# Seven of eight column blocks of each up projection as seven block products

## The reference

```python
def squared_relu_mlp(u, w_up, w_down):
    return jnp.square(jax.nn.relu(u @ w_up)) @ w_down

f = squared_relu_mlp(rmsnorm(h, norm_mlp_pre[i]), w_up[i], w_down[i])
h = h + rmsnorm(f, norm_mlp_post[i])
```

## Time and profile before

| | |
|---|---|
| median of 3 runs | 1296.06 us |
| the profiled execution | 1294.74 us, its span 1293.0 us |
| TensorE matmuls busy | 1281.8 us, 6743 matmuls |
| VectorE, ScalarE, GpSimd busy | 811.8, 656.3, 161.5 us |
| seven blocks of the up projection, layer 0 and 1 | 446.8 to 599.1 and 982.0 to 1134.3 us |
| DMA | 230.01 MB, mean 178 GB/s |

### The profile page before, as it was taken

How to read it: one execution, slowest core, us unless ns; L and a number is a source line. 1 busy time by engine, 2 the same in 40 slices (tenths; PEclk the granted TensorE clock), 3 DMA queues, 4 the chain that set the end, 5 groups by cost and what they waited for, 6 DMA issues and landing times.

```text
span 1293.0 us, 17991 instructions
## 1 busy us (share of the span) xinstructions
PE 1281.8 (99%) x6743; PEld 1058.1 (82%) x6743; DVE 811.8 (63%) x1160; ACT 656.3 (51%) x1141; POOL 161.5 (12%) x195
## 2 busy tenths in 40 slices
PE   9999999999999999999999999999999999999998
PEld 7777878888778988888888898777788888888886
DVE  5676686888544633346787974776374334478887
ACT  6645455677533423235555744775453323365663
POOL 0056353452000000000000000000000000000000
PEclk9999999999999999999999999999999999999999
DMA  7588775354864468858866527646224678669854
GB/s 247 159 269 267 219 180 152 103 165 131 219 155 99 147 198 202 217 170 217 252 207 192 183 83 174 129 108 158 66 82 122 219 182 208 227 189 246 249 173 153
DMA packets 110367, 230.01 MB, mean 178 GB/s; under 512 B 8134, under 2 KB 18646, under 8 KB 110038
## 3 DMA queue, kind: packets, MB, share of 16 engines
q1 hardware_dynamic: 84240, 159.93, 38.0%
q0 software_dynamic: 21760, 67.11, 24.0%
q10 hardware_dynamic: 4294, 2.00, 0.9%
HBM read 225.69 MB, written 70.04 MB: 229 GB/s over the span
## 4 chain that ended last, share of the span: by engine, by line
PE 93%; DVE 3%; DMA 1%; ACT 1%; issue 1%; DVEq 0%; ACTq 0%
PE G L1990 49%; PE G L2417 4%; PE G L2421 4%; PE G L2419 4%; PE X L2013 3%; PE X L2417 3%; PE X L2419 3%; PE X L2421 3%; PE G L2071 3%; PE X L2071 3%; PE X L1990 3%; PE X L2177 1%; PE X L2186 1%; PE X L2260 1%; DVE conv L1433 1%
## 5 line engine op out<-in xcount | busy, mean ns | idle before, releaser
L1296 DVE TENSOR_TENSOR wlo<-raw,whi 128x1024 fp32r<-128x1024 f32 x143 | 176.9, 1237 | 284.3 <-ACT whi L708 284.1
L1990 PE MATMUL G<-uhi,whi 128*128 128x512 f32 x736 | 294.3, 400 | 1.1 <-DVE sz L1421 0.9
L1990 PE MATMUL G<-uhi,wlo 128*128 128x512 f32 x736 | 287.1, 390 | 0.0
L1990 PE MATMUL G<-ulo,whi 128*128 128x512 f32 x736 | 286.7, 390 | 0.0
L708 ACT ACTIVATE whi<-raw 128x1024 fp32r<-128x1024 f32 x143 | 151.6, 1060 | 244.4 <-PE G L1990 159.3
L1118 ACT ACTIVATE whi<-raw 128x1024 fp32r<-128x1024 f32 x112 | 118.5, 1059 | 122.7 <-PE G L2421 52.0
L1764 DVE TENSOR_TENSOR wlo<-raw,whi 128x1024 fp32r<-128x1024 f32 x112 | 135.7, 1223 | 66.0 <-ACT whi L1118 65.6
L1990 PEld LDWEIGHTS G<-uhi,whi 128*128 128x128 f32 x736 | 138.2, 188 | 32.1 <-issue 2.0
L1990 PEld LDWEIGHTS G<-uhi,wlo 128*128 128x128 f32 x736 | 138.1, 188 | 29.6 <-DVE wlo L1344 0.2
L1990 PEld LDWEIGHTS G<-ulo,whi 128*128 128x128 f32 x736 | 138.3, 188 | 28.5
L608 POOL DMA_DIRECT2D tsum<-in_w_down x32 | 32.9, 1038 | 650.2 <-PE G L1990 536.6
(11 more groups left out here) (371 smaller groups left out, 2471.5 us busy)
## 6 DMA issues: line engine op xcount, KB each, us to landing
tsum<-in_w_down POOLq DMA_DIRECT2D x48, 1024.0 KB, 10.4
raw<-in_w_up SPq DMA_DIRECT2D x64, 512.0 KB, 3.9
raw<-tsum SPq DMA_DIRECT2D x64, 512.0 KB, 4.0
raw<-in_w_down SPq DMA_DIRECT2D x48, 512.0 KB, 4.8
raw<-in_ssd_w_in SPq DMA_DIRECT2D x20, 512.0 KB, 4.3
raw<-in_w_mem_kv SPq DMA_DIRECT2D x16, 512.0 KB, 3.7
raw<-in_ssd_w_out SPq DMA_DIRECT2D x16, 512.0 KB, 4.2
raw<-in_swa_w_in SPq DMA_DIRECT2D x16, 512.0 KB, 4.5
```

The costliest lines, as they stand in the source:

```text
L1296: dve.tensor_tensor(wlo[q][:, :, :], src[:, :, :], whi[q][:, :, :].bitcast(F32), ALU.subtract).then_inc(lo_done, 1)
L1990: mm = pe.matmul(o, st, mv, start=(kt == 0 and fresh and not go_on), stop=(q == total - 1 and k == 1), skip_group_check=True)
```

## The change

Seven of the eight column blocks (x = 0 to 6) are done with the same seven products as the down projection: tokens, contraction and columns are halved, so that a product takes 256 tokens, 512 rows and 256 columns of weights, as 2 x 4 x 3 = 24 matmuls with 256 moving columns. The left operand is a quarter of `uhi`/`ulo` for M5, M2, M3 and M6, and for M1, M4, M7 a sum of quarters (`us_parts`), made once a layer from an unsplit copy of u (`u_raw`, copied by ScalarE's `u_copy`); M6's sum is put over the fourth quarter of `uhi`/`ulo`. Sums of weights are made by VectorE in `added` or in place (`up_add`). SyncE loads four quarters of 512 rows x 256 columns a block. Even blocks use the banks G, odd ones X. The first block's relus go straight into `hid` and are squared in place. Panel numbers stay a multiple of four by letting the last product of each odd block count for two. The loads of the gains go out later, in the down products; GpSimd's sums are released at other panel numbers, at nearly the same rate. The diff, cut to its core, goes by engine: names and buffers, SyncE, ScalarE (`u_copy` to the first `up_step`), VectorE (`up_lo` to its own `up_step` and their order), TensorE:

```diff
-UP, PROD, DOWN = 8, 7, 14
-B_KV, N_KV = 39, 23
-B_QA, N_QA = 40, 24
-B_QB, N_QB = 41, 25
-B_Q1, N_Q1 = 42, 26
-B_W1, N_W1 = 43, 27
-B_F1, N_F1 = 46, 29
+PROD, UP, DOWN = 7, 14, 14
+SPLIT = 7
...
+LOADED = {M5: 0, M3: 1, M4: 2}
+ADDED = {M2: 1, M1: 2, M7: 3, M6: 4}
+W_OF, E_OF, E_FULL, W_FULL, C11, C22 = range(1, 7)
+def up_panel(x, r):
+    return 4 + 7 * x + x // 2 + r
+def up_fill(x, r):
+    return 2 if x % 2 and r == PROD - 1 else 1
+def up_next(x, r, n):
+    k = PROD * x + r + n
+    return divmod(k, PROD) if k < PROD * SPLIT else (SPLIT, k - PROD * SPLIT)
...
+        added = put("added", [P, 2, 512], F32, 88)
+        u_raw = [put(f"u_raw{i}", [P, KT, T], F32, (40, 72)[i]) for i in range(2)]
+        us_raw = [[put(f"us_raw{i}{x}", [P, 4, 256], F32, (72, 40)[i] + 4 * x) for x in range(4)] for i in range(2)]
+        us_parts = [[put(f"us{x}{p}", [P, 4, 256], F32R, 8 * x + 4 * p) for p in range(2)] for x in range(3)]
...
+        def up_bank(x, r):
+            return ((X if x % 2 else G)[{M5: 0, M3: 0, M2: 1, M4: 1, M1: 2, M7: 2, M6: 3}[r]])
...
+                def quarter(x, slot, kh, ch):
+                    c0 = 512 * (x + 1) + 256 * ch
+                    src = a["w_up"][i][512 * kh:512 * kh + 512, c0:c0 + 256].rearrange("(k p) n -> p k n", p=P)
+                    sp.dma_start(by_rows(down_raw[slot]), src).then_inc(ring_in[slot], 16)
+                for x in range(SPLIT):
+                    if x == 0:
+                        sp.wait_ge(lo_done, 4 * blk + 1)
+                    else:
+                        sp.wait_ge(up_sum, 28 * i + 4 * (x - 1) + ADDED[M7])
+                    quarter(x, 0, 0, 1)
+                    sp.wait_ge(lo_done, 4 * blk + (3 if x == 0 else up_panel(x - 1, M4) + 1))
+                    quarter(x, 2, 1, 0)
+                    if x == 0:
+                        sp.wait_ge(lo_done, 4 * blk + 2)
+                    else:
+                        sp.wait_ge(up_sum, 28 * i + 4 * (x - 1) + ADDED[M6])
+                    quarter(x, 1, 1, 1)
+                    sp.wait_ge(lo_done, 4 * blk + (4 if x == 0 else up_panel(x - 1, M7) + 1))
+                    quarter(x, 3, 0, 0)
...
+            def u_copy(i, t):
+                act.wait_ge(uhi_ready, U0[2 * i + 2] + 2 * t + 2)
+                act.wait_ge(ulo_ready, U0[2 * i + 2] + 2 * t + 2)
+                for x in range(2):
+                    cp = act.activation(u_raw[i][:, :, P * t + 64 * x:P * t + 64 * x + 64],
+                                        U_BANK[t][x][:, :].rearrange("p (k n) -> p k n", k=KT), ACT.Copy)
+                cp.then_inc(u_raw_done, 1)
...
+                def up_hi(x, r):
+                    n = 4 * blk + up_panel(x, r)
+                    if r in LOADED:
+                        act.wait_ge(ring_in[LOADED[r]], 16 * (23 * i + 2 + x))
+                    else:
+                        act.wait_ge(up_sum, 28 * i + 4 * x + ADDED[r])
+                    act.wait_ge(panel_done, n - 3)
+                    act.activation(by_rows(whi[n % 4]), up_right(r), ACT.Copy).then_inc(hi_done, up_fill(x, r))
...
+                def relu_square(x, th, ch, src):
+                    place = up_out(x, th, ch)
+                    c = 36 * i + 8 + 4 * x + {(0, 1): 0, (1, 0): 1, (0, 0): 2, (1, 1): 3}[th, ch]
+                    act.activation(place, src, ACT.Relu).then_inc(up_relu, 1)
+                    act.wait_ge(up_relu, c - 8 * i - 7)
+                    act.activation(place, place, ACT.Square).then_inc(hidsq_done, 1)
...
+                    nx, nr = up_next(x, r, LOOK)
+                    if nx < SPLIT:
+                        up_hi(nx, nr)
+                    else:
+                        right_hi(nr)
+                    if r == M5 and x > 0:
+                        up_c11_square(x - 1)
+                    elif r == M2:
+                        act.wait_ge(panel_done, 4 * blk + up_panel(x, M5) + 1)
+                        act.activation(up_out(x, 0, 0), up_bank(x, M5)[:, :], ACT.Copy).then_inc(up_m5, 1)
+                        if x > 0:
+                            up_c22_square(x - 1)
+                    elif r == M1:
+                        act.wait_ge(panel_done, 4 * blk + up_panel(x, M3) + 1)
+                        relu_square(x, 0, 1, up_bank(x, M3)[:, :])
+                    elif r == M7:
+                        act.wait_ge(panel_done, 4 * blk + up_panel(x, M4) + 1)
+                        relu_square(x, 1, 0, up_bank(x, M4)[:, :])
...
+                def up_lo(x, r):
+                    n = 4 * blk + up_panel(x, r)
+                    dve.wait_ge(hi_done, n + up_fill(x, r))
+                    dve.tensor_tensor(by_rows(wlo[n % 4]), up_right(r), by_rows(whi[n % 4]).bitcast(F32),
+                                      ALU.subtract).then_inc(lo_done, up_fill(x, r))
+                def up_add(x, r):
+                    b12, b22, b21, b11 = (by_rows(down_raw[y]) for y in range(4))
+                    out_at, other = {M2: (by_rows(added), b21), M1: (by_rows(added), b12), M7: (b11, b12),
+                                     M6: (by_rows(added), b22)}[r]
+                    first = b11 if r == M2 else out_at
+                    for y in {M2: (3, 2), M1: (0,), M7: (), M6: (1,)}[r]:
+                        dve.wait_ge(ring_in[y], 16 * (23 * i + 2 + x))
+                    if r != M2:
+                        dve.wait_ge(up_sum, 28 * i + 4 * x + {M1: 1, M7: 2, M6: 3}[r])
+                    dve.tensor_tensor(out_at, first, other, ALU.add).then_inc(up_sum, 1)
...
+                    nx, nr = up_next(x, r, LOOK)
+                    if nx < SPLIT:
+                        up_lo(nx, nr)
                     else:
-                        dve.wait_ge(panel_done, 4 * blk + 4)
-                    half_relu(1, b, X[b // 2][:, 256 * (b % 2):256 * (b % 2) + 256]).then_inc(half_free, 1)
-                def relus(f, j):
-                    c = 36 * i + 16 * f + 4 * j + 4
-                    for b in range(4):
-                        group_ready(dve, N_F[i] + 4 * f + j, 4 * (blk + 4 * f + j) + 4, b)
-                        dve.wait_ge(hidsq_done, c + b - 1)
-                        dve.tensor_scalar(og[b % 2][:, :], G[b][:, :], 0.0, None, ALU.max).then_inc(bank_free[b], 1)
-                with dve.Fori(1, 4) as j:
-                    ahead(blk + j)
-                    relus(0, j)
+                        right_lo(nr)
+                    w_at, e_at = up_out(x, 0, 0), up_out(x, 1, 1)
+                    before = 4 * blk + up_panel(x, r)
+                    if r == M5 and x > 0:
+                        up_c22_add(x - 1)
+                    elif r == M2:
+                        up_add(x, M7)
+                    elif r == M3:
+                        dve.wait_ge(panel_done, before)
+                        dve.wait_ge(up_m5, 7 * i + x + 1)
+                        dve.tensor_tensor(w_at, up_bank(x, M2)[:, :], w_at, ALU.add).then_inc(up_combined, 1)
+                        up_add(x, M6)
+                    elif r == M1:
+                        dve.wait_ge(up_relu, 28 * i + 4 * x + 1)
+                        dve.wait_ge(up_combined, 42 * i + 6 * x + W_OF)
+                        dve.tensor_tensor(e_at, up_bank(x, M3)[:, :], w_at, ALU.subtract).then_inc(up_combined, 1)
+                    elif r == M4:
+                        dve.wait_ge(panel_done, before)
+                        dve.wait_ge(up_combined, 42 * i + 6 * x + E_OF)
+                        dve.tensor_tensor(e_at, up_bank(x, M1)[:, :], e_at, ALU.add).then_inc(up_combined, 1)
+                        if x + 1 < SPLIT:
+                            up_add(x + 1, M2)
+                    elif r == M7:
+                        dve.wait_ge(up_relu, 28 * i + 4 * x + 2)
+                        dve.wait_ge(up_combined, 42 * i + 6 * x + W_OF)
+                        dve.tensor_tensor(w_at, up_bank(x, M4)[:, :], w_at, ALU.subtract).then_inc(up_combined, 1)
+                    elif r == M6:
+                        dve.wait_ge(panel_done, before)
+                        dve.wait_ge(up_combined, 42 * i + 6 * x + W_FULL)
+                        dve.tensor_tensor(w_at, up_bank(x, M7)[:, :], w_at, ALU.add).then_inc(up_combined, 1)
+                        if x + 1 < SPLIT:
+                            up_add(x + 1, M1)
+                    if x == SPLIT - 1 and r in (M4, M7):
+                        left_parts(M5, r - M4)
+                    if x >= 4 and r == M1:
+                        left_sums(1, x - 4)
...
+                for b in range(4):
+                    dve.wait_ge(half_ready, 8 * i + 2 * (b // 2) + 2)
+                    half_relu(0, b)
+                us_add(1)
+                us_add(2)
+                up_lo(0, M5)
+                up_add(0, M2)
+                up_lo(0, M2)
+                us_lo(M1)
+                up_lo(0, M3)
+                up_add(0, M1)
+                for b in range(4):
+                    if b < 2:
+                        dve.wait_ge(out_ready, 3 * N_F[i] + 2)
```

(87 more changed lines are left out.)

218 lines of the change are left out of this document (133 added, 85 removed).

## The result

| | before | after |
|---|---|---|
| median | 1295.5 us (1294.6 to 1297.4) | 1375.0 us (1372.1 to 1384.7) |
| profiled execution: span | 1293.0 us | 1370.3 us |
| TensorE busy | 1281.8 us, 99% | 1290.2 us, 94% |
| from the split's end to the first down product, layer 0 and 1 | 152.4, 152.4 us | 184.8, 188.3 us |
| down products of layer 0 | 154.1 us | 158.5 us |

The changed kernel is slower: 1.062 times the time before, 95% interval 1.060 to 1.064, that is 79.5 us. The forecast was 1346 us; the time lies within the range, 29 us above the forecast, and most of those 29 us are the rival (c), which had a chance of 0.10.

What follows compares the result with a forecast made beforehand. TensorE was taken as the bound, busy 1281.8 of 1293.0 us. Per layer -11.2 for matmuls, +34.2 for stalls and +2.2 for loads gave +25.2, two layers +50.4, so 1346 us; range 1318 to 1378.

Steps and rivals of the forecast that it cites:

- rival (c): TensorE's clock falls to 1.2 GHz after long stalls: 35 us more, 1381, or 63, about 1410; chance 0.10.
- Matmuls: Up stage: 1176 matmuls a layer at 120 ns, 141.1 us against 152.35, a gain of 11.2 us a layer.
- The chains: Up stage: hand-offs in the program order of VectorE and ScalarE stall TensorE, 34.2 us a layer with restarts.
- Ahead of M7 in blocks 1, 3 and 5: TensorE waits from M4's end for E_FULL, behind up_lo of the next M5: 3.31 us each.
- ahead of M3 in blocks 2, 4 and 6: TensorE waits for ScalarE's copy of M5's bank, behind conversions of M1 and M4: 2.43 us.
- in block 0: First block's stalls: 2.9 us for the copy, 0.2 for W, 3.2 for E_FULL; 6.4 with restarts.
- Loads: Up weight loads, landing at 4.4 us and 6.3 beside sums, add 2.2 us a layer.
- the 5.2 and 9.0: Dearer case for up weight loads, landing at 5.2 us and 9.0 beside sums: some 8.5 us a layer.
- The clock: Up stage: nothing in the trace shows a fall; a fall was priced at one product, 2.88 us; chance 0.10.
- The down products: Gain loads issued there hold up loads wanted two panels of 5.44 us later; costed at nothing.
- Forecast +50.4 in the stage: Both up stages: -11.2 matmuls, +34.2 stalls, +2.2 loads make +25.2 us a layer, two layers +50.4.

Runs made afterwards that it cites:

- e4: Kernel before, with each 512-column matmul in the seven blocks of its up projections cut into two of 256 columns; 1314.4 us, 1.014 of before.
- e3: Changed kernel with E_FULL ahead of up_lo, VectorE's weight sums one step earlier and ScalarE's copy of M5 ahead of up_hi; 1316.4 us, 1.015 of before.
- e5: e3 with GpSimd's twelve transfers beside each up stage cut to 8 of 512 rows, leaving those sums out; 1290.6 us, 0.995 of before.
- e6: e3 with the two gain loads ahead of the 25th weight load of the down products in place of the 9th; 1312.7 us, 1.011 of before.
- e8: e3 with GpSimd's sums moved from beside the up stages to the down products, gain loads ahead of the 41st weight load; 1328.8 us, 1.026 of before.
- e9: e3 with GpSimd's sums spread: eight a layer beside the up stage, eight beside the down products, gain loads later; 1285.3 us, 0.992 of before.
- e1: Changed kernel with VectorE's E_FULL sum ahead of the low parts of the next block's M5; 1350.6 us, 1.043 of before.

## Why the prediction was right and where it was short

**Matmuls: right.** 120 ns in e4 and in the stage after.

**The chains: right in place and size.** Ahead of M7 in blocks 1, 3 and 5 of layer 0 stood 3.22, 3.23 and 3.23 us (3.31 forecast), ahead of M3 in blocks 2, 4 and 6 2.31 (2.43), ahead of M7 in block 2 2.31 (2.4), in block 6 3.08 (3.1), in block 0 2.76, 0.25 and 3.20 (2.9, 0.2, 3.2). The 1.48 us ahead of M3 in block 1 was put at 0.4, and the 0.4 in block 3 did not come. Layer 1 repeats this but for block 0, with 2.12 us ahead of M7 for 3.2, and block 1, with no wait ahead of M3. The sums are 34.2 and 33.7 us against 34.2 for the order and 36.4 with the loads; that the two layers agree so well is in part chance, since layer 1's sum holds 2.9 us of a late load. That the cause is order and not load is shown by e3 and e5.

**Loads: right in sum, in part by luck.** 2.2 us a layer were set, by landing times of 4.4 us at the median and 6.3 beside sums; in layer 0 of the changed kernel they took 5.3 us at the median and 11.7 at most, nearer to the 5.2 and 9.0 that the prediction prices at 8.5 us a layer. Yet late loads lengthened only one gap by 0.9 us in layer 0 (3.97 for 3.1) and one by 2.9 in layer 1 (6.14 for 3.2); in 448 to 594 us ScalarE and VectorE stood 11.1 us for loads, nearly all of it inside gaps that were there anyway. That they would take 8 to 11 us a layer as soon as the order is mended, since a lead of a few us then has to do, the prediction didn't see.

**The clock: the step that failed.** The prediction wrote that nothing in the trace before shows a fall, made it a rival of 0.10, and left it out of the sum. It came behind 14 of the 22 gaps of over 2 us, 22 us in all, most of the miss of 29. The evidence against it was none: no gap of over 1.4 us stood in the trace of before, so it could not speak either way, and the unknown price should have stood in the sum with a bound from both sides. The size was wrong as well, in the other direction: a fall costs 17 steps of 93 ns, 1.6 us, and not the 2.88 of a whole product. So 14 falls gave 22 us, where 12 had been priced at 35. The Trainium skill ("TensorE: Matmul & The Clock Gate", on HAM oscillation) has idle gaps between bursts as its cause; the traces agree, and gaps of 2.1 to 3.2 us, shorter than the waits it shows, were enough here.

**The down products: a wrong cover.** The gain loads were costed at nothing because the weight loads behind them "are wanted two panels of 5.44 us later". A panel there is 2.72 us. What this cost in layer 0 came back in e6 (154.1 against 159.5 us). With the whole slack misread by a factor of two, the same step also led e8 astray.

**4.5 us ahead of the up stage: open.** In the ten traces of after and the experiments that run its split and what lies ahead of it unchanged, the up stage of layer 0 starts at 447.6 to 451.2 us, in the trace of before at 446.8; in e4, which is the kernel before up to there, at 448.3, and in e9, with the whole change in it, at 447.7. So it varies by itself, by more than 3 us under one and the same code; with two traces of the old start on record, what part of it belongs to the change is not shown. In the changed kernel's chain a load of the first stage landed after 11.3 us, 69 us into the span:

```profile
69.30 11.31 DMA raw<-in_ssd_w_in
```

What delayed it wasn't tried.

**In one sum.** Forecast +50.4 in the stage; there came +45.4 (stalls 67.9, matmuls -22.5), and beside it 23.0 of slow clock, 4.5 in the down products, 4.5 ahead of the stage: 77.4.

## What to carry to other kernels

Before splitting work into shorter products, write the engines' queues side by side and ask of each step what the instruction in front of it waits for; busy shares of 80% say nothing, and three moves in program order gave back 59 us here, waits and slow clock together, without one instruction less. Put the clock into the sum too: here about half of TensorE's gaps of 2 to 3 us, and nearly all longer ones, cost some 1.6 us on top. And when waits are mended, look at the transfers next: what had time to spare behind a stall now has to be spaced by hand.

## What the runs showed of the hardware

The distance of matmul starts behind gaps, in the up stages of after and e1 to e3 and e5 to e8, counted from timelines:

| gap, us | gaps | followed by a spell of 213 ns steps |
|---|---|---|
| under 1.9 | 61 | 1 |
| 1.9 to 2.9 | 51 | 28 |
| 2.9 to 3.5 | 16 | 15 |
| over 3.5 | 6 | 6 |

A spell is 12 to 27 steps, mostly 17, and costs 1.1 to 2.5 us, mostly 1.6. It begins at once or up to 13 matmuls after the gap, and the clock then comes back by itself.

GpSimd's copies and sums in DRAM, a megabyte at a time, took 5.8 and 10.3 us in the changed kernel and 13.8 and 16.5 in e8, where they ran beside loads every 2.7 us; beside them a load of half a megabyte went from 5.2 us (6.3 at most, e5) to 7.1 (12.4 at most, e3) in the up stage, and took 14.0 in the down stage of e8.
